# Layer 2 of a four-layer decoder: its gates turned by VectorE and DRAM instead of by TensorE, and its output projection in another order

## The chip, the cores and the metric

One core of a Trainium2 chip runs the whole kernel. The metric is the device time of one execution in microseconds (us), the median of several. TensorE is called PE here, VectorE DVE, ScalarE ACT, GpSimd POOL and SyncE SP; PEld is PE's weight load.

## The reference

Four residual layers over x of 256 rows and 2048 columns, in float32; the layers' mixers are differential attention, sliding-window attention, mLSTM and differential attention again. The change touches the second layer:

```
def sliding_window_attention(h, w_in, w_out, sinks, cos, sin):
    proj = h @ w_in
    q, k, v, g = jnp.split(proj, [SW_WIDTH, SW_WIDTH + nkv, SW_WIDTH + 2 * nkv], axis=-1)
    ...
    e = jnp.exp(s - m)
    p = e / (jnp.sum(e, axis=-1, keepdims=True) + jnp.exp(sk - m))
    o = jnp.einsum('bhgnqk,bnkhd->bnqhgd', p, vv)
    o = o.reshape(B, S, SW_WIDTH) * jax.nn.silu(g)
    return o @ w_out
```

The attention output o comes out of TensorE with the channels on the partitions (transposed); the gate g comes out with the rows of x on the partitions. To multiply them, g has to be transposed (turned). The product is then the input of the output projection.

## The kernel before

**The weights set the pace.** Every projection is cut into jobs of 512 columns, and each job into 8 pairs of 128-row weight chunks. For one pair, SP loads 512 KB into `raw`, ACT rounds it to `w_hi`, DVE computes the rest `w_lo` (L2015), and PE runs 12 matmuls (L1136, L1137, L1138: high times high, low times high, high times low), so that the product is nearly exact. Every engine goes pair by pair: SP loads pair k when PE has finished pair k-8; ACT makes `w_hi` of pair k when PE has finished pair k-4 (the ring of `w_hi` has 8 chunks), and DVE follows ACT. Each engine executes its own list in order, so all side work stands at a hand-written place in it: the tables `SW`, `OUT` and so on give the pair at which a step is done. `w.due(n)` does it at pair n of the iteration, or for n of 16 and above at pair n-16 of the next one.

**Layer 2** (kind `sw`) first makes one job for k and v, then 4 iterations of 2 jobs (16 pairs): one job gives q of 8 heads, the other their gates. The scores (`sc_0`), the softmax, the transposes of the probabilities (`tp`, L1102) and the products with v (`sc_1`) of one iteration lie between the pairs of the same and of the next one. The steps at the place of the change, by their pair in the *next* iteration (number minus 16), are these. DVE makes `gs`, the gate, at 20 (L1821) and scales it by the inverse denominators at 23 and 26 (L1783, two heads' groups). PE turns it after pairs 22 and 24: `g_T`, two blocks of 4 transposes of 128x128, into the two `tp` banks. DVE multiplies at 26 and 28 (`o_gate`, L1792, in place in `th`, which holds o), ACT rounds the product at 27 and 29 (`o_hi`, L986), DVE makes the rest at 29 and 30 (`o_lo`, L1796). At its own pair 11 an iteration turns q on PE; ACT evacuates q (L845) and DVE rotates it (L1560 to L1565) at 11 and 12; ACT copies the turned q at 15 and 16 (`q_hi`, L953), DVE subtracts at 15, 15, 17 and 18 (`q_lo`, L1759), and PE starts the scores of head 0 right after pair 12 (L1209), for which the first `q_lo` must be done. DVE masks and maximises head 0's scores at 16, ACT exponentiates, and PE turns head 0's probabilities after pair 14.

**The output projection** has 4 jobs, each of which accumulates over the 16 chunks of `ot`. Chunks 12 to 15 (pairs 6 and 7 of each job) come from the last iteration, so pairs 0 to 5 of several jobs are done first. `TWO` opens two jobs in the two `acc` banks; pair (0, 6) is then the 13th. `THREE` opens three; (0, 6) is the 19th, and the third job needs a bank of its own (layers 1 and 4 take `tp`). When a job is done, DVE adds it to the residual x and turns it in 32x32 blocks, SP moves it through DRAM, and ACT and DVE split it as the input of the next layer (`sum`, `write`, `read`, `split`).

**A turn through DRAM** exists in the kernel already for q and k of layer 1, for o and for x: one DVE transpose of 128x1024 in 32x32 blocks, 4 DMA writes of 128 KB in 128-byte runs (L566, each waits for nothing but the turn), a wait on SP until they have landed, and one DMA read of 512 KB (L571). All of it goes through the SP queue that also loads the weights.

## Time and profile before

| | |
|---|---|
| median of 3 runs | 1712.66 us (1712.31 to 1713.44) |
| the profiled execution | 1712.57 us |
| its span, first to last instruction | 1710.8 us |
| PE busy | 1699.6 us, 99% |
| PE weight load busy | 1417.7 us, 83% |
| DVE busy | 1188.9 us, 69% |
| ACT busy | 911.4 us, 53% |
| DMA | 364.53 MB, 213 GB/s over the span |
| granted TensorE clock | 0.999 |

A busy time is the union of an engine's instructions. A matmul's own duration (0.39 us for 512 columns) overlaps with its neighbours', so what one costs is read from the distance between starts, not from its duration. The span is cut in the trace by the engines' own lists, and the idle time in front of an instruction is put down to what released it.

### The profile page before, as it was taken

How to read it: one execution, taken by the hardware profiler on the slowest of the kernel's cores; microseconds unless marked ns; L12 is line 12 of the kernel's file. 1: busy time of each engine (PE TensorE's matmuls, PEld its weight loads, DVE VectorE, ACT ScalarE, POOL GpSimd, SP SyncE). 2: the span in 40 equal slices, each digit the busy share in tenths (PEclk: the TensorE clock that was granted, in tenths of full speed). 3: DMA queues.
4: the chain of work that ended last, by engine and by line, in shares of the span. 5: the costliest groups of instructions: out<-in, count | busy, mean ns of one | idle time of the engine just before them, and what ended most of it. 6: DMA issues, size and time to landing. Idle time of an engine off the chain costs nothing.

```text
span 1710.8 us, 24445 instructions
## 1 busy us (share of the span) xinstructions
PE 1699.6 (99%) x7890; PEld 1417.7 (83%) x7890; DVE 1188.9 (69%) x1909; ACT 911.4 (53%) x1400; POOL 38.9 (2%) x99
## 2 busy tenths in 40 slices
PE   9999999999999999999999999999999999999998
PEld 7888888888888888888888888888888888888887
DVE  7767677775769888865656465656676676777756
ACT  7454555554656666655544545454554555455543
POOL 1000000000000000000000000000000000000000
PEclk9999999999999999999999999999999999999999
DMA  8768676766875555478998699966877686767673
GB/s 286 244 194 262 201 245 215 233 216 220 264 216 161 160 159 153 154 234 194 190 166 271 177 201 182 265 182 216 260 227 237 195 265 200 247 214 232 223 237 126
DMA packets 230035, 364.53 MB, mean 213 GB/s; under 512 B 14950, under 2 KB 80044, under 8 KB 229836
## 3 DMA queue, kind: packets, MB, share of 16 engines
q1 hardware_dynamic: 229536, 362.94, 73.5%
q8 instruction: 39, 0.64, 0.2%
q0 software_dynamic: 48, 0.13, 0.1%
q10 hardware_dynamic: 380, 0.56, 0.1%
q14 instruction: 32, 0.26, 0.0%
HBM read 335.79 MB, written 27.79 MB: 213 GB/s over the span
## 4 chain that ended last, share of the span: by engine, by line
PE 95%; DMA 2%; issue 1%; SPq 1%; DVE 1%; ACT 0%; DVEq 0%; POOLq 0%; POOL 0%; ACTq 0%
PE acc L1136 29%; PE acc L1137 29%; PE acc L1138 29%; PE tp L1102 1%; PE tp L1137 1%; PE tp L1136 1%; PE tp L1138 1%; DMA raw<-in_ml_w_in_dram 1%; PE sc L1137 1%; PE sc L1136 1%; PE sc L1138 1%; DMA xres<-in_x_dram 0%; DMA qs<-q_turning 0%; DMA q_turning<-scr 0%; PE sc L1162 0%
## 5 line engine op out<-in xcount | busy, mean ns | idle before, releaser
L2015 DVE TENSOR_TENSOR w_lo<-raw,w_hi 128x1024 fp32r<-128x1024 f32 x583 | 703.2, 1220 | 401.4 <-ACT w_hi L1074 399.0
L1074 ACT ACTIVATE w_hi<-raw 128x1024 fp32r<-128x1024 f32 x583 | 610.2, 1056 | 454.9 <-PE acc L1138 401.6
L1136 PE MATMUL acc<-w_hi,xt_hi 128*128 128x512 f32 x1824 | 715.3, 392 | 1.7 <-DVE w_lo L2015 1.0
L1138 PE MATMUL acc<-w_hi,xt_lo 128*128 128x512 f32 x1824 | 711.0, 390 | 0.0
L1137 PE MATMUL acc<-w_lo,xt_hi 128*128 128x512 f32 x1824 | 710.4, 389 | 0.0
L1138 PEld LDWEIGHTS acc<-w_hi,xt_lo 128*128 128x128 f32 x1824 | 342.4, 188 | 72.3
L1136 PEld LDWEIGHTS acc<-w_hi,xt_hi 128*128 128x128 f32 x1824 | 342.6, 188 | 70.3 <-DVE w_lo L2015 1.6
L1137 PEld LDWEIGHTS acc<-w_lo,xt_hi 128*128 128x128 f32 x1824 | 342.6, 188 | 67.3
L1136 PE MATMUL acc<-w_hi,ot_hi 128*128 128x512 f32 (+1 forms) x456 | 176.6, 387 | 0.0
L1138 PE MATMUL acc<-w_hi,ot_lo 128*128 128x512 f32 (+1 forms) x456 | 175.8, 386 | 0.0
L1137 PE MATMUL acc<-w_lo,ot_hi 128*128 128x512 f32 (+1 forms) x456 | 175.8, 385 | 0.0
L877 ACT ACTIVATE scr<-scr,neg_max_t 128x128 f32<-128x128 f32 (+1 forms) x128 | 57.3, 448 | 95.8 <-DVE neg_max_t L1591 75.6
L1138 PEld LDWEIGHTS acc<-w_hi,ot_lo 128*128 128x128 f32 x456 | 85.7, 188 | 17.2
L1136 PEld LDWEIGHTS acc<-w_hi,ot_hi 128*128 128x128 f32 x456 | 85.7, 188 | 16.8
L1137 PEld LDWEIGHTS acc<-w_lo,ot_hi 128*128 128x128 f32 x456 | 85.7, 188 | 16.7
L805 ACT ACTIVATE junk_x<-xres 128x512 f32<-128x512 f32 x38 | 24.0, 632 | 40.7 <-DVE xres L1980 40.1
L890 ACT ACTIVATE junk_o<-sc 128x256 f32<-128x256 f32 x32 | 12.3, 384 | 37.4 <-PE sc L1138 36.9
L727 POOL TENSOR_TENSOR o_ms<-o_ss,inv 128x2 f32<-128x2 f32 (+1 forms) x20 | 3.9, 197 | 1059.4 <-ACT junk_o L890 1059.4
L863 ACT ACTIVATE th<-acc,rstd_half 128x512 f32<-128x512 f32 x32 | 20.2, 682 | 12.8 <-PE acc L1138 12.8
L845 ACT ACTIVATE qs<-acc,rstd 128x512 f32<-128x512 f32 x32 | 20.3, 684 | 12.3 <-PE acc L1138 12.2
L1636 DVE SCALAR_TENSOR_TENSOR v_lo<-acc,rstd,v_hi 128x512 fp32r<-128x512 f32 x24 | 16.9, 746 | 13.6 <-ACT v_hi L855 13.6
L1136 PE MATMUL tp<-w_hi,ot_hi 128*128 128x512 f32 x64 | 24.9, 389 | 0.0
(306 smaller groups left out, 1226.5 us busy)
## 6 DMA issues: line engine op xcount, KB each, us to landing
raw<-in_da_w_in_dram SPq DMA_DIRECT2D x255, 512.0 KB, 4.4
raw<-in_ml_w_in_dram SPq DMA_DIRECT2D x96, 512.0 KB, 5.7
raw<-in_sw_w_in_dram SPq DMA_DIRECT2D x72, 512.0 KB, 3.7
raw<-in_da_w_out_dram SPq DMA_DIRECT2D x64, 512.0 KB, 4.0
raw<-in_sw_w_out_dram SPq DMA_DIRECT2D x32, 512.0 KB, 3.7
raw<-in_ml_w_in_dram SPq DMA_DIRECT2D x64, 256.0 KB, 7.3
raw<-in_ml_w_out_dram SPq DMA_DIRECT2D x32, 512.0 KB, 3.9
qs<-q_turning SPq DMA_DIRECT2D x12, 512.0 KB, 6.9
```

The source lines that it names most:

```text
L805: act.activation(junk_x[:], xres[:, t, JW * n:JW * n + JW], ACT.Square, accum_out=x_ss[:, t, n:n + 1]).then_inc(sig["x_sq"], 1)
L845: act.activation(dst[:, t], src, ACT.Copy, scale=rstd[:, t:t + 1]).then_inc(act_emptied, 1)
L863: act.activation(dst[:, t, :], acc[b][t][:], ACT.Tanh, scale=rstd_half[:, t:t + 1])\
L877: act.activation(scr[:, slot, cols], scr[:, slot, cols], ACT.Exp, bias=neg_max_t[:, slot, t:t + 1], scale=scale, accum_out=exp_sum[:, slot ...
L890: act.activation(junk_o[:], ml_values(h, t)[:, 0:S] if ml else sc[h][:, S * t:S * t + S], ACT.Square, scale=1.0 if scale is None else scal ...
L1074: act.activation(w_hi[:, q:q + 2, :], raw[:, 2 * p:2 * p + 2, :], ACT.Copy).then_inc(hi_ready, 1)
L1102: m = pe.transpose(dst, src, ident[0:n, 0:n])
L1136: pe.matmul(out_ap, k_hi, m_hi, start=start, stop=False)
L1137: pe.matmul(out_ap, k_hi, m_lo, start=False, stop=False)
L1138: return pe.matmul(out_ap, k_lo, m_hi, start=False, stop=stop)
L1636: dve.scalar_tensor_tensor(lo[:, t], src, rstd[:, t:t + 1], hi[:, t].bitcast(F32), ALU.mult, ALU.subtract)\
L2015: dve.tensor_tensor(w_lo[:, two, :], raw[:, two, :], w_hi[:, q:q + 2, :].bitcast(F32), ALU.subtract).then_inc(lo_ready, 1)
```

## The change

In layer 2 the 8 PE transposes of an iteration are dropped (`g_T`). Instead, at 26, right after the second scaling, DVE turns the whole `gs` in blocks into the score slots 0 to 2 of `scr` (`g_turn`); SP writes them to DRAM at 31, waits there, and reads them back at 31 into slots 3 to 5 (`move_g`). DVE multiplies at 29 and 30 from SBUF, ACT rounds at 30 and 31, DVE makes both rests at 31. The softmax of head 0 in the next iteration waits until the blocks have been written out. For the last iteration, whose gates are finished in the output projection, write and read stand at 33 and 35, and the multiplications, roundings and rests at 33 to 36. The output projection takes the order `THREE`, its third job in the two `sc` banks; its x is summed, moved and split at the places of layers 1 and 4, except that the last job still goes through PE.

```diff
-OUT = {"da": THREE, "sw": dict(TWO, split=(24, 26, 33, 37), turn=(33,)), "ml": TWO}
+OUT = {"da": THREE, "sw": dict(THREE, split=(30, 32, 34, 37), turn=(33,)), "ml": TWO}
...
-          sink=(20, 24), den=(22, 25), g_tanh=19, gate=20, g_scale=(23, 26), g_T=(22, 24),
-          o_gate=(26, 28), o_hi=(27, 29), o_lo=(29, 30))
+          sink=(20, 24), den=(22, 25), g_tanh=19, gate=20, g_scale=(23, 26), g_turn=26,
+          g_write=31, g_write_last=33, g_read=31, g_read_last=35,
+          o_gate=(29, 30), o_gate_last=(33, 34), o_hi=(30, 31), o_hi_last=(34, 35), o_lo=(31, 31), o_lo_last=(35, 36))
...
         def out_bank(l, n):
-            return tp if LAYERS[l][0] == "da" and n == 2 else acc[(OUT0[l] + n) % 2]
+            third = {"da": tp, "sw": sc}.get(LAYERS[l][0])
+            return third if third and n == 2 else acc[(OUT0[l] + n) % 2]
...
+            def move_g(w, l):
+
+                for write_at, read_at, due in ((SW["g_write"], SW["g_read"], w.loop_due),
+                                               (SW["g_write_last"], SW["g_read_last"], w.last_due)):
+                    if (i := due(write_at)) is not None:
+                        write(g_rows, g_blocks, "g_turned", in_iter(l, "g_turned", i, 1), "g_written")
+                    if (i := due(read_at)) is not None:
+                        read(g_landing, g_dram, "g_written", in_iter(l, "g_written", i, 64), "g_moved")
...
-                for b in range(2):
-                    if (i := w.due(SW["g_T"][b])) is not None:
-
-                        pe.wait_ge(sig["g_scaled"], in_iter(l, "g_scaled", i, b + 1))
-                        fill_wait(f"tp_{b}", in_iter(l, f"tp_{b}", i, 5))
-                        for c in range(2):
-                            for t in range(T):
-                                turn(tp[b][:, S * c + P * t:S * c + P * t + P],
-                                     gs[:, t, P * (2 * b + c):P * (2 * b + c) + P], f"tp_{b}" if c + t == 2 else None)
...
+                if (i := w.due(SW["g_turn"])) is not None:
+                    dve.wait_ge(sig["g_scaled"], in_iter(l, "g_scaled", i, 2))
+                    dve.transpose(g_blocks.rearrange("p t j (k n) -> p t k j n", n=32),
+                                  gs[:].rearrange("p t (k j n) -> p t k j n", k=4, j=4)).then_inc(sig["g_turned"], 1)
                 for b in range(2):
                     rows_b = th_rows[:, 2 * b:2 * b + 2, :]
-                    if (i := w.due(SW["o_gate"][b])) is not None:
-                        dve.wait_ge(full[f"tp_{b}"], in_iter(l, f"tp_{b}", i, 6))
+                    if (i := sw_due(w, "o_gate", b)) is not None:
+                        dve.wait_ge(sig["g_moved"], in_iter(l, "g_moved", i, 16))
                         dve.wait_ge(free["sc_1"], in_iter(l, "sc_1", i, 2 + 2 * b))
                         own.wait()
-                        dve.tensor_tensor(th[:, b, :], tp[b][:], th[:, b, :], ALU.mult).then_inc(free[f"tp_{b}"], 1)
+                        o_half = in_blocks(rows_b)
+                        dve.tensor_tensor(o_half, g_landed[:, 2 * b:2 * b + 2], o_half, ALU.mult).then_inc(sig["o_gated"], 1)
...
                         if h == 0:
                             dve.wait_ge(sig["sink_set"], in_iter(l, "sink_set", i, 1))
+                            if not (isinstance(i, int) and i == 0):
+                                dve.wait_ge(sig["g_written"], in_iter(l, "g_written", i, 0))
```

## Rows read from the trace of the kernel before

**Rows 1.** The page, busy shares in 40 slices of the span.

```profile
PE   9999999999999999999999999999999999999998
DVE  7767677775769888865656465656676676777756
PEclk9999999999999999999999999999999999999999
```

**Rows 2.** Waits of PE over the whole span: engine, line, awaited; us, times, longest.

```profile
PE acc L1136 <- DVE w_lo L2015: 1.0, 2, 0.6
PE acc L1136 <- DVE w_lo L2006: 0.8, 1, 0.8
```

**Rows 3.** Windows, the last full iteration of layer 2; columns as printed.

```profile
core 0: us, PE busy (x) PEld busy (x) DVE busy (x) ACT busy (x) POOL busy (x), PEclk, DMA share, GB/s
628.05:682.05 54.00, 54.00 (x273) 45.57 (x272) 47.36 (x113) 36.49 (x74) 0.00 (x0) 1.00 0.54 157
```

**Rows 4.** Timeline of PE at a gate block: start, duration, line, operation.

```profile
558.58 0.39 PE L1138 MATMUL acc<-w_hi,xt_lo 128*128 128x512 f32 x1
558.81 0.60 PE L1102 MATMUL tp<-ident,gs 128*128 128x128 f32 x4
559.16 0.48 PE L1136 MATMUL acc<-w_hi,xt_hi 128*128 128x512 f32 x1
559.48 0.40 PE L1137 MATMUL acc<-w_lo,xt_hi 128*128 128x512 f32 x1
```

**Rows 5.** Timeline of PE, pair 11's end and the first score of an iteration.

```profile
682.10 1.04 PE L1102 MATMUL tp<-ident,qs 128*128 128x128 f32 x8
685.75 0.28 PE L1209 MATMUL sc<-k_all,q_split 128*128 x1
```

**Rows 6.** Timeline of DVE in the same iteration, pairs 10 to 15.

```profile
667.46 0.69 DVE L1792 TENSOR_TENSOR th<-tp,th 128x512 f32<-128x512 f32 x1 [0.24 <-PE tp L1102]
672.76 0.69 DVE L1560 TENSOR_TENSOR shared<-qs,cos_b 128x512 f32<-128x512 f32 x1 [3.02 <-ACT qs L845]
678.80 0.69 DVE L1792 TENSOR_TENSOR th<-tp,th 128x512 f32<-128x512 f32 x1
679.40 1.21 DVE L2015 TENSOR_TENSOR w_lo<-raw,w_hi 128x1024 fp32r<-128x1024 f32 x1
684.45 1.41 DVE L1759 TENSOR_TENSOR q_split<-tp,q_split 64x512 fp32r<-64x512 f32 x2
```

**Rows 7.** Timeline of ACT in the same iteration, pairs 13 to 15.

```profile
679.63 0.64 ACT L986 ACTIVATE ot_hi<-th 128x512 f32 x1 [4.90 <-DVE th L1792]
680.17 1.99 ACT L1074 ACTIVATE w_hi<-raw 128x1024 fp32r<-128x1024 f32 x2
682.07 0.29 ACT L941 ACTIVATE v_hi<-shared 128x128 fp32r x1
682.30 1.06 ACT L1074 ACTIVATE w_hi<-raw 128x1024 fp32r<-128x1024 f32 x1
683.39 1.21 ACT L953 ACTIVATE q_split<-tp 64x512 fp32r<-64x512 f32 x2
```

**Rows 8.** Timeline of SP: pair 15's load; elsewhere four turning writes.

```profile
670.36 0.37 SPq L652 DMA_DIRECT2D raw<-in_sw_w_in_dram  x1
...
752.68 2.56 SPq L566 DMA_DIRECT2D x_turning<-gs  x4
```

**Rows 9.** DMA issues between 750 and 762 us: KB each, us to landing.

```profile
x_turning<-gs SPq DMA_DIRECT2D x4, 128.0 KB, 2.7
th<-x_turning SPq DMA_DIRECT2D x1, 512.0 KB, 5.2
qs<-x_turning SPq DMA_DIRECT2D x1, 512.0 KB, 7.2
```

**Rows 10.** Landing of the one turning read between 473 and 474 us.

```profile
DMA to landing us min/median/max: 3.4/3.4/3.4
```

**Rows 11.** Line L1519, a block transpose of 128x1024: ns min/median/max.

```profile
L1519 DVE STREAM_TRANSPOSE scr<-gs x12: 1245/1246/1248, 136.1 to 1645.0; 128x1024 f32<-128x1024 f32 x12
```

**Rows 12.** Timelines of ACT, DVE and PE where layer 3 takes over.

```profile
783.59 1.69 ACT L820 ACTIVATE xt_hi<-shared,gcol 128x256 fp32r<-128x256 f32 x4
...
797.53 1.66 DVE L1480 SCALAR_TENSOR_TENSOR xt_lo<-tp,gcol,xt_hi 128x256 fp32r<-128x256 f32 x4 [0.62 <-ACT xt_hi L796]
...
799.59 0.28 PE L1235 MATMUL tp<-xt_hi,wg_both 128*32 128x256 f32 x1
```

More of the change, by code:

```diff
@@ L109 @@
     "g_scaled":  ((0, 0, 0), (0, 0, 0), (0, 2, 0), (0, 0, 0)),
+    "g_turned":  ((0, 0, 0), (0, 0, 0), (0, 1, 0), (0, 0, 0)),
+    "g_written": ((0, 0, 0), (0, 0, 0), (0, 64, 0), (0, 0, 0)),
+    "g_moved":   ((0, 0, 0), (0, 0, 0), (0, 16, 0), (0, 0, 0)),
+    "o_gated":   ((0, 0, 0), (0, 0, 0), (0, 2, 0), (0, 0, 0)),
     "x_turned":  ((0, 0, 0), (0, 0, 4), (0, 0, 3), (0, 0, 4)),
@@ L450, in p_parts @@
             return part.rearrange("p h (c i r) -> p (h c) i r", i=4, r=32)
+        g_dram = nc.dram_tensor("g_turning", (P, T * JW), F32, kind="Internal").ap()
+        g_rows = g_dram.rearrange("(j n) (t i r) -> n t j i r", j=4, t=T, i=4)
+        g_blocks = scr_flat[:, 0:T * JW].rearrange("p (t j n) -> p t j n", t=T, j=4)
+        g_landing = scr_flat[:, 3 * BLK:3 * BLK + T * JW]
+        g_landed = g_landing.rearrange("p (a k r) -> p k a r", k=4, r=32)
         def out_bank(l, n):
-            return tp if LAYERS[l][0] == "da" and n == 2 else acc[(OUT0[l] + n) % 2]
+            third = {"da": tp, "sw": sc}.get(LAYERS[l][0])
+            return third if third and n == 2 else acc[(OUT0[l] + n) % 2]
         def x_chunk(n, c):
@@ L511, in wait_emptied, with sw_due @@
             eng.wait_ge(act_emptied if who == "act" else dve_emptied, value)
+        def sw_due(w, what, b):
+            last = w.last_due(SW[what + "_last"][b])
+            return last if last is not None else w.loop_due(SW[what][b])
         def scale_col(l, c2):
@@ L624, in moves @@
                     move_p(w, w.l)
+                if w.kind == "sw":
+                    move_g(w, w.l)
                 move_x(w)
@@ L983, in side_sw_first @@
                 for b in range(2):
-                    if (i := w.due(SW["o_hi"][b])) is not None:
-                        act.wait_ge(free[f"tp_{b}"], in_iter(l, f"tp_{b}", i, 6))
+                    if (i := sw_due(w, "o_hi", b)) is not None:
+                        act.wait_ge(sig["o_gated"], in_iter(l, "o_gated", i, b + 1))
                         act.activation(ot_hi[:, bass.ds(4 * i + 2 * b, 2), :], th_rows[:, 2 * b:2 * b + 2, :], ACT.Copy)\
@@ L1324, in pair @@
                 if p == 0:
-                    if banks is tp:
+                    if banks in (tp, sc):
+                        names = "tp" if banks is tp else "sc"
                         for t in range(T):
-                            fill_wait(f"tp_{t}", in_out(w.l, f"tp_{t}", 0))
+                            fill_wait(f"{names}_{t}", in_out(w.l, f"{names}_{t}", 0))
                     elif w.phase == "iter" and not w.first and j < 2:
@@ L1980, in add_residual @@
                     dve.tensor_tensor(part, part, banks[t][:], ALU.add).then_inc(dve_emptied, 1)
-                if banks is tp:
+                if banks in (tp, sc):
+                    names = "tp" if banks is tp else "sc"
                     wait_emptied(dve, l, OUT0[l] + n)
                     for t in range(T):
-                        dve.sem_inc(full[f"tp_{t}"])
-                        dve.sem_inc(free[f"tp_{t}"])
+                        dve.sem_inc(full[f"{names}_{t}"])
+                        dve.sem_inc(free[f"{names}_{t}"])
                 if not x_kept(l, n):
```

2 lines of the change are left out of this document (1 added, 1 removed), and 8 rows, old and new, of the table COUNTS.

## The prediction

> **What bounds the kernel now.** I read the page first. PE is busy in every slice at full granted clock, DVE is 60 to 90% busy beside it, with its densest slices in layer 2 (slices 12 to 16) [rows 1]. Then I read who makes PE wait: one wait at the start and two short ones elsewhere, 1.8 us together, none of them in layer 2 [rows 2]. The windows say the same of the stage that is changed: an iteration of layer 2 takes 54.0 us, PE is busy in all of it, DVE in 47.36 us, ACT in 36.49 us, the DMA engines for 54% [rows 3]. So the time is the length of PE's list. What is taken off that list is gained in full, unless somebody then makes PE wait. What DVE gets more is free only until a value that PE needs is late; DVE has some 6.6 us of idle time in 54, so places count, not sums. Third, I read the timelines of the iteration boundary, because the new steps all lie there.
>
> **What PE loses.** A block of 4 gate transposes: the matmul in front starts at 558.58, the next two at 559.16 and 559.48 [rows 4]. Without the block, starts would be 0.227 us apart (12 matmuls a pair, 2.73 us), so the second would have started at 559.04. The block costs 0.44 us, or 0.11 us a transpose. There are 2 blocks in 4 iterations: 8 x 0.44 = **3.5 us** less. Nothing covers them, because PE never idles here; from below, PE's matmuls after a block come at 0.23 instead of 0.227 us for a pair, at most 0.04 a block, 0.3 us more.
>
> The Trainium skill (VectorE: DVE Perf Modes, section The three transpose paths) has 390 ns for a 128x128 transpose on TensorE. By that the 32 transposes would give 12.5 us; the starts in the trace, a third of that apart, decide, since the transposes stand in a full pipeline.
>
> **What DVE, ACT and SP get.** DVE: one block transpose more per iteration, 1.25 us [rows 11], at pair 10, where the first `o_gate` goes (0.69 us after 0.24 of waiting) [rows 6]. After that DVE waits 3.02 us for the evacuated q [rows 6], so the difference of 0.3 us is swallowed. The multiplications from SBUF I take at the 0.69 us that they took from PSUM. SP: four write issues, 2.56 us [rows 8], a wait until they have landed, and a read. Behind them in SP's queue stands the load of pair 16, due some 3.3 us after that of pair 15; it goes out about 2 us late, but it is needed by ACT four pairs after it was due, over 10 us, and a turning read of the same size lands in 3.4 to 7.2 us [rows 9, 10]. I cost this at nothing; if SP stood for 8 us, loads would begin to bind. The wait in front of the next softmax is for writes that landed 10 us before: nothing.
>
> **The new chain at the iteration boundary.** This is the term that decides. All times are of the iteration of rows 5 to 8.
> - SP issues pair 15's load at 670.36, when PE has ended pair 7 [rows 8]. The writes follow from 670.8 on; DVE's blocks are ready about 668.5 (667.2, where `o_gate` began to wait, and 1.25) [rows 6, 11]. The fourth write starts at about 672.75 and lands after 2.7 us [rows 9], at 675.45. The read lands 3.4 us [rows 10], 5.2 us or 7.2 us [rows 9] after its issue at 675.5. The last two were taken where loads crowded the queues; here the DMA engines are half idle [rows 3], so I take 4.3, the middle of the first two: the gates are back at **679.8**, and 678.9, 680.7 or 682.7 by the ends.
> - DVE reaches the first `o_gate`, now at pair 13, when pair 12's `w_lo` is done. That one began at 679.40 behind an `o_gate` of 0.6 us that is gone from there [rows 6]: it starts at 678.8 and ends at **679.95**. So the two meet almost at once, at 680.0; DVE waits little.
> - From there the order of the lists makes a chain. `o_gate` 0.69, ACT's `o_hi` 0.6, `w_hi` of pair 14 1.0, the copy of v 0.25, the second `o_hi` 0.6 (its `o_gate` is done by then), `w_hi` of pair 15 1.06, the first `q_hi` 0.6, DVE's first `q_lo` 0.7 [rows 6, 7], and some 0.2 for the handovers: 5.7 us, so 685.7.
> - PE wants that `q_lo` for the first score. It started at 685.75, the q_lo being done at 684.45 + 0.69 = 685.14 [rows 5, 6]; that is 0.6 us of margin. With the block after pair 8 gone, PE comes 0.44 us earlier, at 685.31, and the weights 0.2 before that.
> - So PE waits 0.4 to 0.6 us, say **0.5 us**, in each of the three iterations that have the previous one's gates to finish: **1.5 us** given back. With the read at 5.2 us the chain starts at 680.75: 1.25 us a time, 3.75. Below, with 0.5 us of my chain not there, nothing.
>
> The next thing that could be late is the turning of head 0's probabilities after pair 14: DVE has both q_lo, both rests (2 x 0.6), `w_lo` 15 and the maxima in front of it. By the same durations its exponentials are ready 10.8 us after the chain's start, at 690.8, and PE is there at 692. No wait, with 1.2 us to spare.
>
> The Trainium skill (DMA: Bandwidth & Descriptors, section Specifications) says that transfers under 512 bytes fall below the line rate, which speaks against writing in 128-byte runs; the rows have the price of just these writes, 2.7 us. The same page's section Anatomy of one DMA, whose figures are for DMAs issued by GpSimd, gives a fixed 2.0 us and the bytes at 436 GB/s; an estimate by it is 2.3 us for a write and 3.2 us for the read, the gates back at 678.3, before DVE asks, and the sum as forecast.
>
> **The last iteration and the output projection.** The last gates are written at 33 and read at 35, so the read goes out when PE has finished the 12th pair of the projection, and the 19th needs them, six pairs or 16 us later: free. The third job wants the score banks at its first pair, long after DVE has taken the last product: free. PE makes the same 384 matmuls, into other banks, at the same pace. What moves is the handover to layer 3. The residual sums of jobs 0 and 1 come 6 pairs later, so three turns of x (writes and reads) lie together just when layer 3's loads begin. Layer 1 hands over in this manner and PE never waits there [rows 2]. The margin is thin, though: the gate matmuls of layer 3 start at 799.59, and the last `xt_lo` for them ended at 797.53 + 1.66 = 799.19 [rows 12]. ACT splits the third job one pair later than its 783.59 [rows 12]. If a read lands 2 us later there (7.2 against 5.2 [rows 9]), up to 2.0 - 0.4 = 1.6 us is lost, once. I take 0, and keep 0 to 1.6.
>
> **The sum.** 1712.57 (the profiled execution, 1.8 us of it outside the span) - 3.5 + 1.5 + 0 = 1710.6; that execution lies 0.1 us under the median of 1712.66, so **1710.7 us**, 0.11% faster, which counts as no change: a measurement of this kernel tells about 0.2%, 3.4 us, from nothing.
>
> **The rivals.**
> - *No wait comes back* (26%): the chain is 0.5 us shorter than I added it up, or ACT and DVE overlap more. Then all of 3.5 to 3.8 us is gained: 1708.9 to 1709.2, just past 0.2%. For it: the chain's excess of 0.5 us is no more than its rounding. Against it: every link is a row, and the handovers between engines only add.
> - *The read is late in each iteration* (14%): the one mechanism by which it is slower. The read waits in the queues like the one of 7.2 us [rows 9], the gates land at 682.7, the chain starts at 682.75 and the first score waits 0.5 + 2.75 us three times, 9.75 us: 1712.66 - 3.5 + 9.75 = 1718.9. It loses time from a landing of 5.1 us after issue on (gain and loss are equal where a wait is 1.2 us), and more than 0.2% from about 6.3 us on (a wait of 2.3 us). Against it: the queues hold only pair 15's load.
> - *The handover to layer 3 is late* (10%): 1.6 us on top of the forecast, 1712.3.
> - *The transposes were not PE's time* (2%): PE waits for something else in their place, and nothing is gained: 1712.7 and above.
>
> The forecast itself, 0.2 to 1.25 us a wait, 1709.3 to 1712.9, has 48%. Faster is the first rival, 0.26; slower the second, 0.14; within 0.2% the other three, 0.60. The range: low 1708.6, the first rival's end with the slower pace after a block counted; high 1715.0, which takes in a read of 5.2 us (1712.9) with a late handover (1.6) and leaves out most of the second rival.
>
> **What would show it.** Right: no L1102 with `gs` on PE in layer 2 except a small one of layer 3; an iteration of 53.1 us plus the wait; PE idle once per iteration, in front of L1209 or its weight load, put down to DVE's `q_split`; the turning read landing 3.4 to 5.2 us after issue; DVE idle under 1 us before the first `o_gate`. Wrong: PE waits for `w_lo` in pairs 13 to 16 or for the exponentials (DVE, not the chain, is the bound), raw loads that make ACT wait, or iterations of 53.1 us with no wait at all. What would break the prediction is a read that takes over 6.3 us here, or a PE wait at a place that I counted as free.

## The result: 2.6 us slower, within 0.2%, and just outside the range

| | before | after |
|---|---|---|
| median of 22 runs | 1712.78 us (1711.03 to 1713.74) | 1715.37 us (1713.94 to 1717.28) |
| span of the profiled execution | 1710.8 us | 1714.1 us |
| PE busy | 1699.6 us | 1698.7 us |
| DVE busy | 1188.9 us | 1193.2 us |
| ACT busy | 911.4 us | 910.5 us |

The ratio is 1.0017, with an interval of 1.001 to 1.0023. Of the three outcomes it is "within 0.2%", the likeliest of the forecast; but the forecast was 1710.7 us, 2 us under the median of before, with a range up to 1715.0. The changed kernel is 0.4 us above the range, and the interval leaves no room for a gain.

The page of the kernel after, its size and the busy shares that answer to [rows 1]:

```profile
span 1714.1 us, 24405 instructions
PE 1698.7 (99%) x7858; PEld 1415.6 (83%) x7858; DVE 1193.2 (70%) x1913; ACT 910.5 (53%) x1400; POOL 37.7 (2%) x99
PE   9999999999999999999999999999999999999998
DVE  7768677775759888956656465656766676777756
PEclk9999999999999999999999999999999999999999
```

The clock is the same. PE lost only 0.9 us of busy time, and the last of DVE's five dense slices (the 13th to the 17th; the prediction's "12 to 16" counts from 0) is denser than before. The waits of PE (engine, operands, line, whom it awaited; us, times, longest) are the view to begin with, against [rows 2]:

```profile
PE acc L1164 <- DVE w_lo L2043: 2.1, 2, 1.0
PE tp L1254 <- DVE xt_lo L1500: 1.8, 1, 1.8
PE sc L1237 <- DVE row_max L1601: 1.5, 3, 0.5
PE sc L1237 <- DVE q_split L1779: 0.9, 3, 0.4
```

Three of these are new. L1237 is a head's first score matmul. It waits three times for `q_split`, DVE's `q_lo`: this is the wait that was predicted. It waits three times for `row_max`: DVE's maxima (L1601) had not yet emptied the score bank. And the gate matmuls of layer 3 wait once, 1.8 us, for `xt_lo`. A wait in this list is only the idle time; what a late engine costs is read from the distance of starts.

The iteration that answers to [rows 3], in the same stretch of time:

```profile
628.05:682.05 54.00, 53.20 (x264) 44.32 (x263) 48.06 (x114) 35.93 (x73) 0.00 (x0) 1.00 0.58 173
```

PE has 9 records fewer here (the 8 transposes among them) and idled for 0.8 us, and DVE has 0.7 us more work. The starts of the first score matmul of each iteration, taken from PE's timeline (before 523.73, 577.73, 631.74, 685.75; after 524.50, 577.93, 632.25, 686.70), give the iterations: 54.0 us each before; 53.4, 54.3 and 54.5 after. 54.0 less the two blocks would be 53.1. The first of them has a new wait only at its end (no earlier iteration's gates lie at its start); the other two give the whole gain back, with more.

**Where the time went.** From the first score to the transposes of x for layer 3 (PE's last block of the layer, at 795.95 before, 796.76 after) the layer takes 272.22 us before and 272.26 us after: nothing gained. From there to the first gate matmul of layer 3 (799.59 before [rows 12]) it takes 3.64 us before and 5.59 us after: **1.95 us lost**. PE's timelines, the first line before, the others after:

```profile
795.95 1.04 PE L1102 MATMUL tp<-ident,xres 128*128 128x128 f32 x8
796.76 1.03 PE L1130 MATMUL tp<-ident,xres 128*128 128x128 f32 x8
802.35 0.28 PE L1254 MATMUL tp<-xt_hi,wg_both 128*32 128x256 f32 x1 [1.81 <-DVE xt_lo L1500]
```

The rest of the difference of the two spans (3.3 us) is 0.8 us at the start of the kernel, which varies among executions (the first score began between 523.2 and 525.1 in the runs below), and 0.5 us in layer 3, nearly all of it between 220 and 320 us behind its first gate matmul. There PE of both kernels waits for `w_lo`: the two waits of the first row above lie there, and the two at L2015 in [rows 2]. ACT, which stands in front of DVE, waits there for the weights from DRAM (ACT's waits of the kernel after, 1025 to 1095 us):

```profile
ACT w_hi L1102 <- DMA raw<-in_ml_w_in_dram: 26.7, 17, 2.9
```

A second execution of the kernel after (`after_again` below) is only 0.1 us longer than before in all that follows the gate matmuls, so these 0.5 us are not shown to be the change's. The medians, which average over the start, differ by 2.6 us.

**The boundary of an iteration, after.** DVE's timeline (start, duration, line, operation, count; in brackets the idle time before it and who ended it), the same boundary as [rows 6]. In this execution the whole layer lies later; the load of pair 15, which was at 670.36 in [rows 8], is issued at 671.25:

```profile
679.71 1.22 DVE L2043 TENSOR_TENSOR w_lo<-raw,w_hi 128x1024 fp32r<-128x1024 f32 x1
680.94 0.69 DVE L1817 TENSOR_TENSOR th<-scr,th 128x512 f32<-128x512 f32 x1
681.54 1.22 DVE L2043 TENSOR_TENSOR w_lo<-raw,w_hi 128x1024 fp32r<-128x1024 f32 x1
682.68 0.68 DVE L1817 TENSOR_TENSOR th<-scr,th 128x512 f32<-128x512 f32 x1
683.38 1.23 DVE L2043 TENSOR_TENSOR w_lo<-raw,w_hi 128x1024 fp32r<-128x1024 f32 x1
685.74 1.41 DVE L1779 TENSOR_TENSOR q_split<-tp,q_split 64x512 fp32r<-64x512 f32 x2 [0.94 <-ACT q_split L981]
687.18 1.30 DVE L1821 TENSOR_TENSOR ot_lo<-th,ot_hi 128x512 f32 x2
688.39 1.22 DVE L2043 TENSOR_TENSOR w_lo<-raw,w_hi 128x1024 fp32r<-128x1024 f32 x1
689.64 0.29 DVE L1596 TENSOR_TENSOR scr<-sc,masks 128x128 f32<-128x128 f32 x1
```

PE's timeline at the first and the second score:

```profile
686.70 0.38 PE L1237 MATMUL sc<-k_all,q_split 128*128 x1 [0.39 <-DVE q_split L1779]
690.54 0.39 PE L1237 MATMUL sc<-k_all,q_split 128*128 x1 [0.47 <-DVE row_max L1601]
```

One chain runs through both. DVE waits 0.94 us for ACT's copy of q (because ACT has the second `o_hi` in front of it), makes two `q_lo`, and the first of these starts the first score. From there to 690.4 DVE never stops: two `q_lo`, two `o_lo`, a `w_lo`, and only then head 0's maxima, which free the bank that head 1's score goes into. The first and the second score start 3.84 us apart, where before it was 3.10 to 3.11 (685.75 [rows 5] and this line of the kernel before):

```profile
688.85 0.28 PE L1209 MATMUL sc<-k_all,q_split 128*128 x1
```

Before, the maxima began 2.7 us after the first `q_lo` (687.14 and 684.45), because neither `o_lo` stood between them; after, 3.9 us.

### The profile page after: what moved, and what is told of

The parts are those of the page before. It is cut to its first block, busy times and chain, and to the rows that moved or that the text cites. A ratio compares the mean times of both kernels' runs of the same rounds, so it can differ in the third digit from the quotient of the medians.

```text
span 1714.1 us, 24405 instructions
## 1 busy us (share of the span) xinstructions
PE 1698.7 (99%) x7858; PEld 1415.6 (83%) x7858; DVE 1193.2 (70%) x1913; ACT 910.5 (53%) x1400; POOL 37.7 (2%) x99
## 4 chain that ended last, share of the span: by engine, by line
PE 92%; DVE 2%; DMA 2%; issue 2%; ACT 1%; SPq 1%; DVEq 0%; ACTq 0%; POOLq 0%; POOL 0%
PE acc L1164 28%; PE acc L1165 28%; PE acc L1166 28%; PE sc L1165 1%; PE sc L1164 1%; PE sc L1166 1%; PE tp L1164 1%; PE tp L1165 1%; PE tp L1166 1%; PE tp L1130 1%; DMA raw<-in_ml_w_in_dram 1%; DVE w_lo L2043 1%; ACT w_hi L1102 1%; DMA shared<-x_turning 0%; PE sc L1190 0%
## 5 line engine op out<-in xcount | busy, mean ns | idle before, releaser
L1164 PE MATMUL acc<-w_hi,ot_hi 128*128 128x512 f32 (+1 forms) x424 | 163.9, 387 | 0.0
L1165 PE MATMUL acc<-w_lo,ot_hi 128*128 128x512 f32 (+1 forms) x424 | 163.3, 385 | 0.0
L1166 PE MATMUL acc<-w_hi,ot_lo 128*128 128x512 f32 (+1 forms) x424 | 163.3, 385 | 0.0
L1166 PEld LDWEIGHTS acc<-w_hi,ot_lo 128*128 128x128 f32 x424 | 79.6, 188 | 16.1
L1164 PEld LDWEIGHTS acc<-w_hi,ot_hi 128*128 128x128 f32 x424 | 79.7, 188 | 15.6
L1165 PEld LDWEIGHTS acc<-w_lo,ot_hi 128*128 128x128 f32 x424 | 79.7, 188 | 15.4
```

The source lines that it names most:

```text
L1164: pe.matmul(out_ap, k_hi, m_hi, start=start, stop=False)
L1165: pe.matmul(out_ap, k_hi, m_lo, start=False, stop=False)
L1166: return pe.matmul(out_ap, k_lo, m_hi, start=False, stop=stop)
```

## The experiments

After the first look, the theory was: **two waits per iteration, both made by the order of ACT's and DVE's lists in pairs 13 to 16, eat what PE was relieved of; and the order `THREE` costs 1 to 2 us once, at the handover to layer 3.** The rivals: the trip through DRAM (its landing, or SP standing still) is what makes the loop's waits; one part of the change alone makes all of the loss; the eight blocks were never worth 3.5 us. Each kernel was timed 11 times against the kernel before on the same chip (33 runs for each group):

| kernel | median, us | before there | ratio (interval) |
|---|---|---|---|
| `three_only` | 1713.89 | 1712.56 | 1.0009 (1.0 to 1.0018) |
| `loop_only` | 1713.19 | 1712.56 | 1.0003 (0.9994 to 1.0012) |
| `max_early` | 1715.23 | 1712.56 | 1.0016 (1.0006 to 1.0025) |
| `hi_late` | 1713.27 | 1712.56 | 1.0005 (0.9996 to 1.0014) |
| `gates_later` | 1713.64 | 1712.18 | 1.0007 (0.9998 to 1.0016) |
| `no_moves` | 1714.34 | 1712.18 | 1.0013 (1.0004 to 1.0023) |
| `lo_on_pool` | 1715.87 | 1712.18 | 1.002 (1.0011 to 1.0029) |
| `three_places` | 1710.52 | 1712.18 | 0.9989 (0.998 to 0.9998) |
| `after_again` | 1714.62 | 1712.23 | 1.0016 (1.0006 to 1.0025) |
| `no_turns` | 1709.58 | 1712.23 | 0.9985 (0.9976 to 0.9994) |
| `loop_places` | 1709.69 | 1712.23 | 0.9986 (0.9977 to 0.9995) |
| `three_places_again` | 1710.06 | 1712.23 | 0.9987 (0.9978 to 0.9996) |

An interval is some 1.5 us to either side, so single medians separate only the larger steps. Therefore each verdict rests on distances within one trace too: the iterations, the distance from the first to the second score (3.1 us where nothing waits), the layer (first score to the transposes of x; 272.22 us before), and the handover (from there to the first gate matmul; 3.64 us before). There is one trace of each run. The edits of `three_only` and `no_turns` are shown against the kernel before, all others against the kernel after.

### The two parts alone

`three_only` is the kernel before with the order `THREE`, its third job in the score banks; the gates stay on PE.

```diff
-OUT = {"da": THREE, "sw": dict(TWO, split=(24, 26, 33, 37), turn=(33,)), "ml": TWO}
+OUT = {"da": THREE, "sw": dict(THREE, split=(30, 32, 34, 37), turn=(33,)), "ml": TWO}
...
-            return tp if LAYERS[l][0] == "da" and n == 2 else acc[(OUT0[l] + n) % 2]
+            third = {"da": tp, "sw": sc}.get(LAYERS[l][0])
+            return third if third and n == 2 else acc[(OUT0[l] + n) % 2]
```

> The kernel before with the output projection of layer 2 in the order THREE and its third job in the score banks; the gates are still turned on PE. Theory (the handover to layer 3 costs PE one wait of 1.95 us at the gate matmuls of layer 3, as in the trace of the changed kernel, and the order costs nothing else): 1.9 to 2.0 us slower than before, some 1714.7, the only new wait of PE being that one, behind DVE's xt_lo. Rival 1 (the order is the whole loss, with costs that the waits don't show): 5 us or more slower. Rival 2 (the late handover comes from the turned gates, not from the order): the same as before.

Measured: 1.3 us slower in the medians; the layer takes 272.23 us, as before, and the handover 5.24 us, 1.6 us more. One wait of it is new:

```profile
PE tp L1236 <- DVE xt_lo L1482: 1.4, 1, 1.4
```

`loop_only` is the other half: the first three iterations' gates go through DRAM, the last iteration's are turned by PE as before, and the order stays `TWO`.

```diff
-OUT = {"da": THREE, "sw": dict(THREE, split=(30, 32, 34, 37), turn=(33,)), "ml": TWO}
+OUT = {"da": THREE, "sw": dict(TWO, split=(24, 26, 33, 37), turn=(33,)), "ml": TWO}
...
-                for write_at, read_at, due in ((SW["g_write"], SW["g_read"], w.loop_due),
-                                               (SW["g_write_last"], SW["g_read_last"], w.last_due)):
+                for write_at, read_at, due in ((SW["g_write"], SW["g_read"], w.loop_due),):
...
+            def g_T(w, l):
+                for b in range(2):
+                    if (i := w.last_due(SW["g_T"][b])) is not None:
...
```

> The changed kernel with its DRAM turn for the first three iterations only; the last iteration's gates are turned on PE, and the output projection keeps the order TWO in the acc banks. Theory (6 blocks of 0.44 us go, and each of three iterations waits 0.3 us for the first q_lo and 0.8 us for the score bank that the maxima of head 0 empty, with 0.1 us behind it, 3.65 us in all): 1.0 us slower than before, 1713.8, the next layer's gate matmuls without a wait. Rival (the waits in the loop are small, the order is the loss): 2.0 to 2.6 us faster than before, 1710.2 to 1710.8.

Measured: 0.6 us slower, and both waits of the loop are there; the handover takes 3.64 us, exactly that of before.

```profile
PE sc L1239 <- DVE row_max L1615: 1.6, 3, 0.5
PE sc L1239 <- DVE q_split L1793: 0.8, 3, 0.3
```

So the two losses belong to two parts, and neither part explains the other's. By the traces they add up: the layer is 0.96 us longer than before with the loop alone (273.18 us), 0.92 us of that comes back when the last iteration's two blocks go too, and the handover adds 1.6 to 2.0. The rival "one part makes all of it" has fallen.

### The handover, by itself

`gates_later`: the kernel after, with layer 3's gate matmuls one pair later on PE.

```diff
-                if w.idx == 2:
+                if w.idx == 3:
```

> The changed kernel with the gate matmuls of layer 3 behind its fourth pair instead of its third. Theory (the order THREE brings the last part of x 2 us too late for just these matmuls, and nothing else there is short): that wait goes, 1.9 to 2.0 us faster than the changed kernel, 1713.4. Rival (the lateness is DVE's and ACT's in general and goes on to w_lo): the wait moves behind one for w_lo, the same 1715.4.

Measured: 1713.64 us, 1.5 us slower than before where the kernel after is 2.4 to 2.6 slower. The wait for `xt_lo` is gone from the list; the gate matmuls come 6.33 us after the transposes of x, that is 3.64 and one pair (2.73), so nothing waits there any more. The loop's waits are unchanged (distance of the scores 3.87 us). The median moved less than the 1.95 us of the trace, but the intervals are wide enough for both.

Why `xt_lo` is late is seen in ACT's timeline of the kernel after, against [rows 12]: what it waits for before each split of x.

```profile
778.24 1.71 ACT L848 ACTIVATE xt_hi<-th,gcol 128x256 fp32r<-128x256 f32 x4 [0.27 <-DMA th<-x_turning]
785.00 1.71 ACT L848 ACTIVATE xt_hi<-qs,gcol 128x256 fp32r<-128x256 f32 x4 [3.16 <-DMA qs<-x_turning]
790.60 1.71 ACT L848 ACTIVATE xt_hi<-shared,gcol 128x256 fp32r<-128x256 f32 x4 [1.99 <-DMA shared<-x_turning]
799.14 1.57 ACT L824 ACTIVATE xt_hi<-tp,gcol 128x256 fp32r<-128x256 f32 x4
```

And the reads of x in the DMA issues between 755 and 800 us (KB, us from issue to landing):

```profile
th<-x_turning SPq DMA_DIRECT2D x1, 512.0 KB, 4.9
qs<-x_turning SPq DMA_DIRECT2D x1, 512.0 KB, 5.4
shared<-x_turning SPq DMA_DIRECT2D x1, 512.0 KB, 7.5
```

The third split was at 783.59 before and is at 790.60 now. Behind it in DVE's list stand its `xt_lo`, a `w_lo` and the last job's sum (794.43 instead of 790.70), and behind that ACT's squares and two `w_hi`: the fourth split, the one through PE, begins at 799.14 instead of 796.59, and its `xt_lo` ends at 802.2 instead of 799.19. The lateness of a DMA at 783 thus reaches PE at 802, through 19 us of lists in fixed order.

Why the third read lands late is seen in SP's timeline, two lines before and two after:

```profile
771.54 2.56 SPq L566 DMA_DIRECT2D x_turning<-shared  x4
776.36 0.47 SPq L571 DMA_DIRECT2D shared<-x_turning  x1
776.29 3.22 SPq L583 DMA_DIRECT2D x_turning<-shared  x4
783.07 0.34 SPq L588 DMA_DIRECT2D shared<-x_turning  x1
```

From the first of the four writes to the landing of the last it took 4.4 us before (771.54 to 775.93) and takes 6.8 us after (776.29 to 783.05), and the read goes out only then. The read itself took 6.9 us before already, and takes 7.5. Of the third split's lateness, 2.4 us are therefore the writes' and 0.6 the read's. The writes are those that follow another turn closely; that this is why they take longer is likely, but no run separates the turns.

### The loop: the trip through DRAM, or the lists?

`no_moves`: the kernel after without the four writes, the read and the waits for them.

```diff
-                if w.kind == "sw":
-                    move_g(w, w.l)
...
-                        dve.wait_ge(sig["g_moved"], in_iter(l, "g_moved", i, 16))
...
-                            if not (isinstance(i, int) and i == 0):
-                                dve.wait_ge(sig["g_written"], in_iter(l, "g_written", i, 0))
```

> The changed kernel without the four writes and the read of the turned gates, and without the waits for them; the block transpose stays, and o is multiplied by what lies in the landing place, so the output is not the layer's. Theory (the waits in the loop come from work that was put into DVE's dense stretch between q's rotation and the scores, not from the moves, since the gates land when DVE gets there): the same two waits of 0.3 and 0.8 us, the same time as the changed kernel, at most 0.5 us less by the handover. Rival (the landing, or the moves' traffic, is what makes the chain late): the waits in the loop go, 3.6 us faster, 1711.8.

Measured: 1714.34 us, and the same two waits in each iteration:

```profile
PE sc L1235 <- DVE row_max L1599: 1.6, 3, 0.5
PE sc L1235 <- DVE q_split L1777: 1.4, 3, 0.6
```

The scores stand 3.87 us apart as in the kernel after, and the waits for `q_lo` are not shorter but a little longer (0.4 to 0.6 us; the kernel after has 0.3 to 0.4), for which I have no reason. So neither the landing of the gates nor SP's waiting is needed for them: the DMA rival has fallen. The DMA issues of the kernel after between 670 and 682 us say the same:

```profile
g_turning<-scr SPq DMA_DIRECT2D x4, 128.0 KB, 3.4
scr<-g_turning SPq DMA_DIRECT2D x1, 512.0 KB, 4.0
```

The read is issued at 676.92 and lands 4.0 us later, at 680.9; DVE, its `w_lo` done, starts the multiplication at 680.94 and has no wait in front of it.

`max_early`: the maxima of head 0 moved in front of the two `o_lo`, at pair 15 behind the first two `q_lo`.

```diff
+                if (i := w.due(SW["max_first"])) is not None:
...
+                    row_maxima(l, i, 0, 0, 0, in_iter(l, "sc_0", i, 0), mask_sw)
...
-                    if (i := w.due(SW["softmax"] + h)) is not None:
+                    if h and (i := w.due(SW["softmax"] + h)) is not None:
```

> The changed kernel with DVE's mask and maxima of head 0 moved from pair 16 to pair 15, right behind the first two q_lo and ahead of both o_lo and of pair 15's w_lo. Theory (PE's second score waits for a bank that stands behind 2.4 us of other DVE work): the wait on row_max goes, 0.8 us in each of three iterations, 2.3 us faster than the changed kernel, 1713.1; the wait on the first q_lo, 0.3 us, stays. Rival (DVE is full there, the place doesn't matter): the wait turns up elsewhere, at w_lo or at a later score, and the time stays at 1715.4.

Measured: 1715.23 us, no gain. The second score no longer waits (3.18 us behind the first), but the third does (4.00 us behind the second):

```profile
693.10 0.39 PE L1237 MATMUL sc<-k_all,q_split 128*128 x1 [0.72 <-DVE row_max L1601]
```

One step put ahead of the others does not help: the two `o_lo` and pair 15's `w_lo` now stand between head 0's maxima and head 1's, and the wait went to the next customer of the same list. At its new place DVE even idles 0.32 us, because the score itself is not there yet; the iterations take 54.5 us, 0.1 to 0.2 more than in the kernel after.

`hi_late`: ACT makes the second `o_hi` only behind `w_hi` of pair 15 and the copies of q.

```diff
+                if (i := sw_due(w, "o_hi", 1)) is not None:
+                    act.wait_ge(sig["o_gated"], in_iter(l, "o_gated", i, 2))
+                    act.activation(ot_hi[:, bass.ds(4 * i + 2, 2), :], th_rows[:, 2:4, :], ACT.Copy).then_inc(sig["t_hi"], 1)
...
-                for b in range(2):
+                for b in range(1):
                     if (i := sw_due(w, "o_hi", b)) is not None:
```

> The changed kernel with ACT's second o_hi moved behind pair 15's w_hi and the first q_hi. Theory (the wait on the first q_lo is the chain o_gate, o_hi, w_hi, o_hi, w_hi, q_hi, q_lo; 0.6 us shorter, it is under the margin, and DVE reaches the maxima 0.3 to 0.6 us earlier too): the wait of 0.3 us goes and the one of 0.8 us shrinks to 0.2 to 0.5, 1.8 to 2.7 us faster over three iterations, 1712.7 to 1713.6. Rival (the chain starts with a late landing of the gates, DVE waits for it): the same as the changed kernel.

Measured: 1713.27 us, 0.7 slower than before instead of 2.4 to 2.6. The wait for `q_split` is gone, as PE's waits show, and DVE (its timeline below) waits 0.34 us for ACT's copy of q where it was 0.94:

```profile
PE sc L1240 <- DVE row_max L1604: 1.3, 3, 0.5
```

```profile
682.65 1.41 DVE L1782 TENSOR_TENSOR q_split<-tp,q_split 64x512 fp32r<-64x512 f32 x2 [0.34 <-ACT q_split L981]
```

The iterations take 53.7 us instead of 54.3 to 54.5. That is the first of the two waits; the second is left, the scores 3.69 us apart.

`three_places`: the second `o_hi` late, the gate matmuls of layer 3 one pair later, and the first `o_lo` at 30, so that DVE makes it before `w_lo` 14, ahead of its idle time, and not behind `q_lo`. The edit of this third move (the other two are those of `hi_late` and `gates_later`):

```diff
-          o_gate=(29, 30), o_gate_last=(33, 34), o_hi=(30, 31), o_hi_last=(34, 35), o_lo=(31, 31), o_lo_last=(35, 36))
+          o_gate=(29, 30), o_gate_last=(33, 34), o_hi=(30, 31), o_hi_last=(34, 35), o_lo=(30, 31), o_lo_last=(35, 36))
```

> The changed kernel with three steps at other places: ACT's second o_hi behind the first q_hi, the gate matmuls of layer 3 one pair later, and DVE's first o_lo at pair 14, where DVE idles 0.9 us before the first q_lo, instead of at 15. Theory: the first two bring 2.1 us (as measured for the first alone) and 1.9 us, the third 0.3 to 0.6 us per iteration of the 0.6 us that are left on row_max: 1715.4 - 2.1 - 1.9 - 0.9 to 1.8 = 1709.6 to 1710.5, which would be 2 to 3 us faster than the kernel before. Rival (DVE is full, the earlier o_lo brings back the wait on the first q_lo as long as it shortens the other): 1711.4.

Measured: 1710.52 us, **1.7 us faster than the kernel before** (interval 0.3 to 3.4), where the kernel after is 2.4 to 2.6 slower. PE's waits for `q_split`, `row_max` and `xt_lo` have all left the list. The iterations take 53.07, 53.28 and 53.27 us. DVE at the same boundary:

```profile
679.36 0.68 DVE L1824 TENSOR_TENSOR ot_lo<-th,ot_hi 128x512 f32 x1
679.96 0.69 DVE L1820 TENSOR_TENSOR th<-scr,th 128x512 f32<-128x512 f32 x1
680.56 1.22 DVE L2046 TENSOR_TENSOR w_lo<-raw,w_hi 128x1024 fp32r<-128x1024 f32 x1
681.70 0.28 DVE L1767 TENSOR_TENSOR v_hi<-shared,v_hi 128x128 fp32r<-128x128 f32 x1
682.01 1.41 DVE L1782 TENSOR_TENSOR q_split<-tp,q_split 64x512 fp32r<-64x512 f32 x2
```

No idle time is left in front of `q_lo`. The operations are the same as in the kernel after. Of the 0.94 us idle there, ACT's earlier copy of q has taken 0.6 away (`hi_late`), and an `o_lo` that used to stand behind `q_lo` fills the rest, so the maxima begin 3.3 us after the first `q_lo` (at 685.31) where it was 3.9. The scores stand 3.27 us apart, still 0.16 more than before, in pieces too short for the list of waits. The `o_lo` was never moved alone; its share is the step from 3.69 us (`hi_late`) to 3.27.

### DVE relieved by POOL

`lo_on_pool`: both `o_lo` of all four iterations are made by POOL, which has nothing else to do in this layer.

```diff
-                        dve.tensor_tensor(ot_lo[:, chunk, :], rows_b, ot_hi[:].bitcast(F32)[:, chunk, :], ALU.subtract)\
-                           .then_inc(sig["ot_done"], 1)
...
+                            pool.tensor_tensor(ot_lo[:, chunk, :], th_rows[:, 2 * b:2 * b + 2, :],
+                                               ot_hi[:].bitcast(F32)[:, chunk, :], ALU.subtract)\
+                                .then_inc(sig["ot_done"], 1)
```

> The changed kernel with both o_lo of an iteration on POOL, which is idle in layer 2, instead of on DVE. Theory (PE's second score waits because DVE has too much between the first q_lo and the maxima of head 0, the two o_lo being 1.2 us of it): the wait on row_max, 0.8 us in each iteration, goes, the one of 0.3 us on the first q_lo stays: 2.3 to 2.6 us faster than the changed kernel, 1712.8 to 1713.1. Rival (the next link takes its place: w_lo or the maxima of head 1, as when the maxima of head 0 were moved): less than 1 us faster.

Neither the theory nor its rival came true. Measured: 1715.87 us, the slowest of these kernels. DVE had 1.3 us less to do per iteration, and the wait for `row_max` is indeed gone, but the first score now waits up to 1.5 us:

```profile
PE sc L1244 <- DVE q_split L1786: 4.4, 3, 1.5
```

The timelines of POOL and of DVE, at the same place:

```profile
682.61 1.33 POOL L774 TENSOR_TENSOR ot_lo<-th,ot_hi 128x512 f32 x1 [50.62 <-ACT ot_hi L1021]
685.46 1.30 POOL L774 TENSOR_TENSOR ot_lo<-th,ot_hi 128x512 f32 x1 [1.52 <-ACT ot_hi L1021]
```

```profile
680.97 0.68 DVE L1824 TENSOR_TENSOR th<-scr,th 128x512 f32<-128x512 f32 x1
682.71 1.77 DVE L1824 TENSOR_TENSOR th<-scr,th 128x512 f32<-128x512 f32 x1
685.54 1.37 DVE L1771 TENSOR_TENSOR v_hi<-shared,v_hi 128x128 fp32r<-128x128 f32 x1
```

The same multiplication takes DVE 0.68 us alone and 1.77 us when POOL had begun 0.1 us before it; the copy of v takes 1.37 us instead of 0.28. Both end about when POOL has ended and their own time has passed (683.94 + 0.68 is 684.6, against 684.5; 686.76 + 0.28 is 687.0, against 686.9). DVE has lost 2.2 us in front of `q_lo` and been spared 1.3 behind it. I had counted POOL's work as free because POOL is idle.

### What the blocks are worth, and which version is best

`after_again` is the kernel after, unchanged, to compare it on this chip.

> The changed kernel itself, beside the others of this group and the kernel before on one chip. By its trace it should be 3.65 (waits of the loop) + 1.95 (handover) - 3.5 (blocks) = 2.1 us slower than before; the first measurement said 2.6. All other runs of this group are read against this one.

Measured: 1714.62 us, 2.4 us slower than before, with the same three new waits (handover 5.20 us in this trace, 1.6 us more than before).

`no_turns` is the kernel before without the eight blocks, everything else at its place; o is multiplied by the gate as it lies.

```diff
-                for b in range(2):
-                    if (i := w.due(SW["g_T"][b])) is not None:
...
-                        dve.tensor_tensor(th[:, b, :], tp[b][:], th[:, b, :], ALU.mult).then_inc(free[f"tp_{b}"], 1)
+                        dve.tensor_tensor(th[:, b, :], gs[:, b, :], th[:, b, :], ALU.mult).then_inc(sig["o_gated"], 1)
```

> The kernel before with PE's gate blocks left out and nothing in their place: o is multiplied by the gate as it lies in gs, not turned, so the output is not the layer's; all places and the order TWO are as before. Theory (PE's list is the time, 8 blocks at 0.44 us): 3.5 us faster than before, no new wait. Rival (the margin of 0.6 us in front of the first score is used up, since PE comes 0.44 us earlier): 2 to 3 us faster with a wait in front of the scores. Rival 2 (the blocks were not PE's time): the same as before.

Measured: 2.65 us faster than before, interval 1.0 to 4.1. The windows show an iteration with PE busy throughout:

```profile
630.09:683.39 53.30, 53.30 (x264) 44.70 (x265) 47.24 (x113) 36.33 (x73) 0.00 (x0) 1.00 0.52 157
```

The first iteration is 0.86 us shorter, as two blocks of 0.44 say; the next two only 0.67 and 0.70, of which 0.11 lies at the second score (3.22 us behind the first instead of 3.11). The whole layer is 3.05 us shorter (269.17 us). So in the layer the blocks were worth about 3 us, not 3.5. (From the first score to the end of the trace the kernel is 4.0 us shorter; the other 0.9 lies in the stretch of layer 3 named above, where PE idles 0.6 us instead of 1.4.)

`loop_places` is `loop_only` (order `TWO`, the last iteration on PE) with the two moves of `three_places` that concern the loop. `three_places_again` repeats `three_places` beside it.

```diff
-          o_gate=(29, 30), o_gate_last=(26, 28), g_T=(22, 24), o_hi=(30, 31), o_hi_last=(27, 29), o_lo=(31, 31), o_lo_last=(29, 30))
+          o_gate=(29, 30), o_gate_last=(26, 28), g_T=(22, 24), o_hi=(30, 31), o_hi_last=(27, 29), o_lo=(30, 31), o_lo_last=(29, 30))
...
-                for b in range(2):
+                for b in range(1 if w.phase == "iter" else 2):
                     if (i := sw_due(w, "o_hi", b)) is not None:
```

> The kernel with the DRAM turn in the loop alone (last iteration on PE, order TWO), with the second o_hi behind the first q_hi and the first o_lo at pair 14. By what the traces of the others show: 6 blocks of 0.44 us less, 0.25 us of waiting in each of three iterations, no change at the handover: 2.6 - 0.75 = 1.9 us faster than before. Rival (the order THREE and the late gate matmuls are needed for the gain): the same as before.

> The changed kernel with the second o_hi, the first o_lo and the gate matmuls of layer 3 at other places, once more, beside the others: by its trace 8 x 0.44 - 3 x 0.25 = 2.8 us faster than before; the first measurement said 1.7 (0.3 to 3.4). If it is not faster than loop_places by about 0.9 us (the last iteration's two blocks), something at the handover is still paid that the waits don't show.

Measured: 1709.69 us and 1710.06 us, 2.5 and 2.2 us faster than before. `loop_places` has iterations of 53.03, 53.31 and 53.28 us and a handover of 3.64 us; none of the new waits is left. It has the lowest median of the versions that do all of the layer's work, beats both kernels, and needs neither the new order of the projection nor the moves of the last gates. The last iteration's two blocks are 0.9 us of PE's list, and `three_places_again` should have shown them, but it is 0.4 us behind, in medians that are uncertain by 1.5.

The traces say where they went. From the first score to the end of the trace it is 1187.1 us before, 1183.8 and 1183.9 in the two executions of `three_places`, and 1183.9 with `loop_places`: 3.1 to 3.3 us less, and no difference between the two versions. In the layer `three_places` is 1 us ahead (3.1 us shorter than before, against 2.1). In layer 3 it falls back, in the stretch where ACT waits for the weights from DRAM: from the first score of its third iteration to that of the fourth it takes 92.8 us in both its executions and 91.9 with `loop_places` (92.2 before). What makes the weights late there, and whether the order `THREE` or the moves of the last gates have a part in it, no run shows.

## Why the prediction was wrong, step by step

- **PE's list shortens by 3.5 us.** Nearly right. Alone, the removal is worth 3.05 us by the trace and 2.65 by the medians. The 0.44 us of a block holds (first iteration of `no_turns`); the 0.3 us that the prediction would have added for the pace after a block did not come, and 0.45 us less was gained than 8 blocks say. The Trainium skill (VectorE: DVE Perf Modes, section The three transpose paths) gives 390 ns for a transpose of 128x128 in bf16 on TensorE. Inside this stream of float32 matmuls the figure does not hold: it would have given 12.5 us, and the removal brought about 3.
- **The gates are back in time.** Right. Predicted 9.4 us after the load of pair 15 is issued, measured 9.7 (671.25 to 680.9). DVE was predicted to arrive 9.6 after it, and arrived at 9.7. The writes took longer than the 2.7 us assumed (3.0 to 3.9), the reads in the loop 3.3 to 4.0 instead of 4.3. The estimate by the Trainium skill (DMA: Bandwidth & Descriptors, section Anatomy of one DMA), gates back at 678.3, was 1.7 us too early once the start is shifted by 0.9.
- **The chain of 5.7 us, and the first score's wait of 0.5 us.** Right, the wait 0.2 us too large. Measured 5.8 us from the first multiplication to the first score (680.94 to 686.70), 0.39 us of waiting in that row, 0.3 on average. `hi_late` shows the mechanism: with one `o_hi` taken out of ACT's part of the chain the wait is gone.
- **"The next thing that could be late is the turning of head 0's probabilities."** This is the step that failed. The list of DVE's work in front of the maxima was written down in full ("both q_lo, both rests, `w_lo` 15 and the maxima"), but held only against the consumer of the exponentials, after pair 14. The maxima have an earlier consumer: they empty the score bank, and head 1's score wants it one pair after head 0's (a `fill_wait` on `sc_0`, a few lines above the matmul of L1209). The prediction's own durations would have given it, as an estimate: the first `q_lo` done at 685.7, then 0.7 (`q_lo`), 1.2 (rests), 1.2 (`w_lo`) and 0.8 for the maxima (687.14 to 687.98 in the trace of before) make 689.6, and head 1's score is due 3.1 us after head 0's, at 688.8: a wait of 0.8 us. Measured, it cost 0.76 us at the second score (3.87 us instead of 3.11) and about 0.1 at the restart, three times: 2.6 us. `no_moves` shows that the DMA is not needed for it, `max_early`, `hi_late` and `three_places` that DVE's stretch and its order make it.
- **The handover at 0, with "0 to 1.6" as a rival of 10%.** The second step that failed. The rival's price came true: 1.6 us in the trace of `three_only`, 1.95 in that of after, 1.4 to 2.2 in the seven traces with the order `THREE` and the gate matmuls at their old place. Its mechanism was half right. It had one read that lands in 7.2 instead of 5.2 us; but the third read took 6.9 us before already and only 0.6 more after, and the larger part, 2.4 us, is in the four writes in front of it, which the prediction did not price there. So the size of 1.6 us was in part luck. The margin of 0.4 us had been read, beside reads of 5.2 and 7.2 us on the same path; three turns close together were reason enough to doubt it. "Layer 1 hands over in this manner" was no evidence for a margin of another size.
- **The last iteration and the score banks are free.** Right. DVE waits 1.3 us for the last gates' read (5.2 us to its landing), and PE never for DVE there; `three_only` shows no wait for the banks.
- **The rivals.** "No wait comes back" and "the read is late in each iteration" did not happen; "the transposes were not PE's time" is refuted by `no_turns`.

The sum with what was measured, in the layer and at the handover: -3.5 (the blocks) + 3 x 1.2 (both scores and the restart) + 1.95 = +2.1 us, against +2.6 in the medians. The 0.5 us of layer 3 in this trace would close the gap, but the second execution of the same kernel has 0.1 there, so what is left stays open; it is less than the medians' uncertainty. The range failed because its upper end was made of the two doubts I had seen; the term that was missing had no place in it.

## What to carry to other kernels

When a step is made later in an engine's list, follow each later step of that list to *all* its customers: those that read its result and those that wait for the buffer or bank that it empties. The earliest of them decides. If a stretch of the engine is full, moving one step ahead only moves the wait to the next customer (`max_early`); the repair is to put work into idle time in front of the stretch (`three_places`). A margin of 0.4 us behind a DMA whose rows read 5.2 and 7.2 us is no margin.

## What the hardware showed that I had not expected

An idle POOL is not free for elementwise work beside DVE. While a POOL operation of 1.3 us on SBUF ran, DVE operations with two SBUF inputs took 1.77 instead of 0.68 us and 1.37 instead of 0.28 us. The Trainium skill says the same (SBUF — State Buffer, section SBUF: two separate sides): DVE and GpSimd have a port pair in common that is locked, not divided, so that a DVE operation with two SBUF inputs is held for the whole of a GpSimd operation that reads SBUF and began before it. These rows agree, to 0.15 us.

The 128 KB writes of the gates in 128-byte runs landed 3.0 to 3.9 us after their issue in the loop, and those of x for layer 3 up to 5.1, where the same kind took 2.7 us in [rows 9]. Reads of one size, 512 KB, landed in 3.3 to 7.9 us within the one execution of the kernel after. The longest of x, 7.5 us, had layer 3's loads about it, but `loop_only` has one of 8.3 us (758.87) before those loads had begun (776.24), so they are not needed for a long read. Two or three rows of one path do not bound what it can take.
